# A two-block model on one core: both attentions, the first output product and the state-space outputs in another order

## The reference

```
proj = rms_norm(x) @ w_in;  q, k, v, p = split(proj)            # 8 heads of 128
a = attention(norm(q), norm(k), v, rel_bias)                    # per head
m = mean of p over the last 2, 4, 8, 16 tokens, minus p; @ pool_w; * pool_scale
x = x + concat(a, m) @ w_out                                    # "mix"
x = x + (silu(conv(h @ w_up)[gate]) * conv(h @ w_up)[val]) @ w_down
h = concat(meta, x)                                             # 16 + 256 = 272 tokens
y_a = rmsnorm((ssd forward + ssd backward + D * xs) * silu(z))  # 8 groups of 4 heads
y_b = silu(layernorm(conv31(val * sigmoid(gate)))) * silu(z_b)
h = h + concat(y_a, y_b) @ w_out_2                              # "outa", then "outb"
q, k, v, z = split(rmsnorm(h) @ w_in_o)                         # 32 heads of 64
h = h + (neighbourhood_attention(q, k, v) * silu(z)) @ w_out_o  # "na", then "naout"
out = rmsnorm(h)[meta:]
```

## Time and profile before

| | us |
|---|---|
| three runs, median | 2695.35 |
| the profiled execution, its own time | 2695.7 |
| its span, first to last instruction | 2693.8 |
| PE busy | 2558.0 |
| DVE busy | 1909.6 |
| ACT busy | 1142.4 |
| POOL busy | 408.3 |

### The profile page before, as it was taken

How to read it: one execution, slowest core, us unless ns; L and a number is a source line. 1 busy time by engine, 2 the same in 40 slices (tenths; PEclk the granted TensorE clock), 3 DMA queues, 4 the chain that set the end, 5 groups by cost and what they waited for, 6 DMA issues and landing times.

```text
span 2693.8 us, 57478 instructions
## 1 busy us (share of the span) xinstructions
PE 2558.0 (95%) x19902; PEld 2449.2 (91%) x19902; DVE 1909.6 (71%) x3412; ACT 1142.4 (42%) x1603; POOL 408.3 (15%) x261
## 2 busy tenths in 40 slices
PE   5998999999999999999989899996989999999997
PEld 4997999999999999999977799996989988888887
DVE  5767767777777555588889888888766656666655
ACT  3443344444444444433366533333334433444433
POOL 0000000000000000020057487771000000000100
PEclk7999999999999999999999999997999999999999
DMA  5454455555556566655544355552455544444443
GB/s 209 158 165 138 149 179 187 187 185 185 185 186 198 180 186 182 190 173 164 179 140 143 122 180 172 175 183 95 147 160 158 177 148 136 154 144 150 141 130 131
DMA packets 160394, 441.00 MB, mean 164 GB/s; under 512 B 39248, under 2 KB 56016, under 8 KB 159968
## 3 DMA queue, kind: packets, MB, share of 16 engines
q1 hardware_dynamic: 157760, 431.48, 50.4%
q0 software_dynamic: 2592, 8.98, 1.2%
HBM read 436.67 MB, written 11.08 MB: 166 GB/s over the span
## 4 chain that ended last, share of the span: by engine, by line
PE 78%; DVE 11%; issue 5%; ACT 4%; DVEq 1%; DMA 0%; ACTq 0%; SPq 0%
PE bank L831 24%; PE bank L832 24%; PE bank L833 24%; ACT whi L511 2%; DVE c L1463 2%; PE bank L1083 2%; DVE wlo L1153 2%; PE bank L1068 1%; DVE eb L1536 1%; ACT eb L675 1%; PE bank L1074 1%; DVE pad L1164 0%; DVE c L1461 0%; PE bank L999 0%; ACT sq L520 0%
## 5 line engine op out<-in xcount | busy, mean ns | idle before, releaser
L831 PE MATMUL bank<-xh,whi 128*128 128x256 f32 (+1 forms) x4496 | 1303.7, 290 | 47.4 <-DVE wlo L1153 27.0
L832 PE MATMUL bank<-xl,whi 128*128 128x256 f32 (+1 forms) x4496 | 1286.3, 286 | 0.0
L833 PE MATMUL bank<-xh,wlo 128*128 128x256 f32 (+1 forms) x4496 | 1286.0, 286 | 0.0
L511 ACT CAST whi<-raw 128x1024 fp32r<-128x1024 f32 x785 | 811.4, 1044 | 658.4 <-PE bank L833 628.5
L1153 DVE TENSOR_TENSOR wlo<-raw,whi 128x1024 fp32r<-128x1024 f32 x689 | 843.6, 1234 | 271.2 <-ACT whi L511 256.0
L831 PEld LDWEIGHTS bank<-xh,whi 128*128 128x128 f32 x4496 | 854.9, 190 | 77.9 <-issue 43.8
L833 PEld LDWEIGHTS bank<-xh,wlo 128*128 128x128 f32 x4496 | 855.1, 190 | 0.0
L832 PEld LDWEIGHTS bank<-xl,whi 128*128 128x128 f32 x4496 | 852.7, 190 | 2.2 <-issue 1.9
L831 PE MATMUL bank<-fh,whi 128*128 128x256 f32 x960 | 271.8, 283 | 0.3 <-DVE fl L1338 0.3
L832 PE MATMUL bank<-fl,whi 128*128 128x256 f32 x960 | 271.7, 283 | 0.0
L833 PE MATMUL bank<-fh,wlo 128*128 128x256 f32 x960 | 271.7, 283 | 0.0
(11 more groups left out here) (280 smaller groups left out, 2813.5 us busy)
## 6 DMA issues: line engine op xcount, KB each, us to landing
raw<-w_up SPq DMA_DIRECT2D x176, 512.0 KB, 4.0
raw<-w_na SPq DMA_DIRECT2D x128, 512.0 KB, 3.8
raw<-w_glu SPq DMA_DIRECT2D x96, 512.0 KB, 3.5
raw<-w_down SPq DMA_DIRECT2D x80, 512.0 KB, 4.2
raw<-w_qkvp SPq DMA_DIRECT2D x64, 512.0 KB, 4.1
raw<-w_xbc SPq DMA_DIRECT2D x64, 512.0 KB, 4.1
raw<-w_mix SPq DMA_DIRECT2D x32, 512.0 KB, 3.9
raw<-w_za SPq DMA_DIRECT2D x32, 512.0 KB, 3.8
```

What stands on the lines that cost most here:

```text
L511: A.copy(whi[s][:, :], raw[s][:, :]).then_inc(sem("hi_done"), 1)
L831: T.matmul(out, wh, mh[:, o:o + n], start=start and r == 0, stop=False)
L832: T.matmul(out, wh, ml[:, o:o + n], start=False, stop=False)
L833: ins = T.matmul(out, wl, mh[:, o:o + n], start=False, stop=stop and r == len(kts) - 1)
```

## The change

On PE, the stream of small and large matmuls is rebuilt in both attentions and in `outa`; other engines follow it.

- `p` has a phase of its own ahead (`pin`), and `qkv` now has 6 chunks per head. POOL makes the windowed means during `qkv` and carries the bias rows through memory; their products with `pool_w` stand in the last two heads. The last head's attention stands between the first chunks of `mix`, which begin with the half of the inputs that comes from the means.
- In `mix`, `down` and `naout` the high weights are multiplied with both parts of the activations by one matmul of 512 columns; the two halves of the bank are added by DVE (one more `TENSOR_TENSOR` per output tile).
- `outputs`, `nscores` and `nvalues` alternate between the two heads. All four scores of a pair stand together (after chunk 0), all transposes (after chunk 4) and all values (after chunk 6).
- `outa`: four banks in turn instead of two; POOL splits its weights; DVE's and ACT's share is written out as a list for 16 tiles, with the layernorm's gain and bias taken into ACT's instruction.
- The last pair's attention stands between the first chunks of `naout`.

What the change does to the streams is shown at three places. PE in the loop over pairs of the neighbourhood attention, before: values of the first head, then the transposes of the second (`nps` are probabilities, `nvr` values, `nsc` scores; the square bracket is what an instruction waits for).

The diff, cut to its core:

```diff
@@ on SP and POOL: the bias table and the windowed means
-            sp.wait_ge(sem("brow_ready"), HEADS)
-            sp.dma_start(brows[:, :], btab[:, :]).then_inc(sem("brow_out"), 16)
...
+            pool.wait_ge(sem("brow_ready"), HEADS)
+            G.dma_start(brows[:, :], btab[:, :]).then_inc(sem("brow_out"), 16)
...
+            def window(out, src, lo_, shift, so, ss):
+                gch.link(G.tensor_tensor(p3(out, lo_, 8, META, TOK, so), p3(src, lo_, 8, META, TOK, ss),
+                                         p3(src, lo_, 8, META - shift, TOK - shift, ss), ADD))
...
+            with pool.Fori(0, 4) as i:
+                for j in range(8):
+                    split("outa", i, j)
@@ in product, for mix, down and naout
-                    T.matmul(out, wh, mh[:, o:o + n], start=start and r == 0, stop=False)
-                    T.matmul(out, wh, ml[:, o:o + n], start=False, stop=False)
-                    ins = T.matmul(out, wl, mh[:, o:o + n], start=False,
-                                   stop=stop and r == len(kts) - 1)
+                    if phase in ("mix", "down", "naout"):
+                        both = pb_[:, 0:2 * n].rearrange("p (t n) -> p t n", t=2)
+                        if not last:
+                            T.matmul(both, wh, halves(mh, ml, o, n), start=head, stop=False)
+                        ins = T.matmul(out, wl, mh[:, o:o + n], start=False, stop=False)
+                        if last:
+                            ins = T.matmul(both, wh, halves(mh, ml, o, n), start=False, stop=True)
+                        continue
@@ on PE: qkv, the last head and mix
+                    if jj == 0 and attn:
+                        turn_values(i * 2 + m, i, 3 * m - 1)
+                    if jj == 1 and attn:
+                        scores(i * 2 + m)
...
+            mixing(0, 0, range(8, 16), start=True)
+            turn_values(8, 3, 5)
+            pe.wait_ge(sem("bank_free"), tile("mix", 0, 1) + 1)
+            mixing(1, 0, range(8, 16), start=True)
             scores(8)
+            pe.wait_ge(sem("vq_ready"), 8)
+            mixing(2, 0, range(8, 16), bank[2], start=True)
+            mixing(3, 0, range(8, 16), bank[7], start=True)
             turn_probs(8)
+            pe.wait_ge(sem("y_ready"), 7)
+            mixing(0, 1, range(7), done=False)
             values(8)
@@ on PE: the outputs of the state-space scan
-                for h in range(2):
-                    for n, (t0, o, w_) in enumerate(YSEGS[d]):
+                for n, (t0, o, w_) in enumerate(YSEGS[d]):
+                    for h in range(2):
@@ on PE: outa
-            outa(0)
-            pe.wait_ge(sem("ln_acc"), 2 + 16)
+                    if begin and j == 0:
                         pe.wait_ge(sem("lsum_ready"), 1)
+                        T.matmul(mean, ones[:, :], lsum[:, :], start=True,
                                  stop=True).then_inc(sem("mean_done"), 1)
+            outa(0, True)
+            pe.wait_ge(sem("lacc_ready"), 1)
@@ on DVE: outa
+            for n in range(16):
+                difference(n)
+                if n > 1:
+                    summed(n - 2)
+                if n in (4, 10):
+                    added(n // 6)
...
+            for n, upto in zip(range(2, 16), (0, 1, 3, 5, 6, 8, 9, 11, 12, 13, 14, 15, 16, 16)):
+                while at_ < upto:
+                    branch(at_)
+                    at_ += 1
+                added(n)
@@ on DVE: the residual of mix, down and naout
+                    if phase != "outb":
+                        ch.link(V.tensor_tensor(xt, from_[:, n:2 * n], xt, ADD))
+                    freed(phase, i, k, V.tensor_tensor(xt, from_[:, 0:n], xt, ADD))
@@ on PE: the neighbourhood attention
+            def nscores(i):
+                pe.wait_ge(sem("bank_free"), tile("na", i, 0) + 2)
+                for m in range(4):
+                    b_, h = divmod(m, 2)
+                    o = 64 * h
+                    T.matmul(bank[3 + m][:, 0:TOK], qt[o:o + 64, b_ * P:b_ * P + P], kt_[o:o + 64, :],
+                             start=True, stop=True).then_inc(sem("nscores_done"), 1)
...
+                for n in range(3):
+                    for h in range(2):
+                        ins = T.matmul(bank[7][64 * h:64 * h + 64, 0:SEQ],
+                                       nvr[:, n * P + 64 * h:n * P + 64 * h + 64],
+                                       nps[h][:, n * SEQ:n * SEQ + SEQ], start=n == 0, stop=n == 2)
...
                     if attn and j == 0:
+                        nscores(i)
+                    if attn and j == 4:
+                        nturn(i)
+                    if attn and j == 6:
+                        nvalues(i)
```

More of the change, by code:

```diff
@@ L547, in residual @@
                 else:
-                    with act.Fori(0, 8) as i:
+                    with act.Fori(2 if phase == "mix" else 0, 8) as i:
                         body(i)
@@ L820, in _, with halves, product @@
             pe.sem_inc(sem("chunk_done"), RING)
-            def product(phase, i, j, k, mh, ml, kts, width, off, n, start, stop):
-                if start:
+            def halves(mh, ml, o, n):
+                h, l = mh[:, o:o + n], ml[:, o:o + n]
+                return bass.AP(tensor=h.tensor, offset=h.offset,
+                               ap=[h.ap[0], [l.offset - h.offset, 2], [1, n]])
+            def product(phase, i, j, k, mh, ml, kts, width, off, n, start, stop, to=None, done=True):
+                if start and phase not in ("mix", "outa", "naout"):
@@ L1341, in _ @@
-            dve.wait_ge(sem("bank_free"), tile("pool", 0, 7) + 3)
-            for n in range(8):
-                dve.sem_inc(sem("y_ready"), 1)
+            with dve.Fori(1, 3) as i:
+                ch.begin(i, 14, 1)
+                qkv(i)
+            ch.end(2)
+            qkv(3, pooled=True)
+            ch.end()
+            split("mix", 0, 0)
+            normalized(8)
+            head_out(7)
+            split("mix", 0, 1)
+            values_in(8)
+            softmax_in(8)
+            split("mix", 0, 2)
@@ L1344, in _ @@
+            softmax_out(8)
+            split("mix", 0, 3)
+            split("mix", 1, 0)
+            head_out(8)
+            split("mix", 1, 1)
             ch.end()
```

767 lines of the change are left out of this document (438 added, 329 removed).

## The result

| | before | after |
|---|---|---|
| device time, median of 4 runs | 2695.05 us | 2583.66 us (2581.68 to 2586.24) |
| ratio to before, 95% interval | | 0.9588 (0.9571 to 0.9604) |
| profiled execution, span | 2695.7, 2693.8 us | 2586.24, 2584.4 us |
| predicted | | 2568 (2542 to 2602) |

The account below looks back on a forecast made before the run. PE bounds the kernel, busy 2558.0 of 2693.8 us. Terms -17 - 13.5 - 16 + 1.3 - 1 - 34 - 39 - 8 = -127 from 2695.7 give 2568 us, range 2542 to 2602.

Parts of the forecast that it names:

- Start and first attention to mix: Up to the first sum of squares -17 us (bounds -10, -21); first attention to `mix` -13.5 (bounds -5, -17).
- POOL has made the means during the first heads: First attention to `mix`: the means are off DVE's chain by then; part of the -13.5 us.
- Wide matmul: `mix`, `down`, `naout`: one 512-column matmul for two of 256 gains 13.5 ns a pair, -16 us in all.
- State-space outputs: State-space scan: alternating heads saves perhaps 0.15 us a call over 32 calls; -1 us (bounds 0 and -5).
- what PE saves it then waits: State-space scan: PE waits for DVE, busy 20.63 of 23.40 us a group, so the saving turns into waiting; -1 us.
- outa: First output product: of 46.1 us lost 12 stay, with 7.9 waiting for the sum; -34 us (bounds -20, -38).
- POOL keeps up with a fifth to spare: `outa`: POOL's split takes 2.40 us against 3.02 for a chunk.
- Pairs: Neighbourhood attention: values 1.3, scores 0.9, merging 0.4, so 2.6 us a pair over 15 pairs; -39 (bounds -20, -45).
- Last pair: Last pair's attention between chunks of `naout`, which cover most of the softmax; -8 us (bounds -3 and -9).
- 1.6 stays: Last pair: DVE has some 7.8 us from the first score on, PE has 6.2; 1.6 us of loss remains.
- The shorter heads wait: Rival, first attention: DVE 2 us late in each of 8 heads, 16 us more, 2584; chance 0.12.
- The halves don't overlap: Rival, pairs: only the 0.4 us of a pair is left, 33 us more, 2601; chance 0.08.

Follow-up runs that it names:

- e5: The changed kernel with the windowed means left out, POOL's semaphores kept; single run 2580.51 us.
- e7: The changed kernel with other banks and bank waits in `mix` and `naout`, and the splits of `mix` chunks 9 and 10 moved ahead; 2573.38 us.
- e1: The changed kernel with the state-space outputs run head by head again, not alternating; 2585.09 us.
- e6: The changed kernel with two buffers exchanged in `outa`: the layernorm's running value in PSUM, the gate's output in SBUF; 2582.37 us.
- e11: The changed kernel with all gaining edits together, plus ACT's splits of `outa`'s fourth to sixth chunk ahead of its norm; 2554.08 us.
- e3: The changed kernel with a pair's four score matmuls issued head 0, 0, 1, 1, not alternating; 2586.1 us.
- e8: The changed kernel with the windowed means spread: POOL waits for three more splits of `qkv` before each of twelve portions; 2581.25 us.

## Why the prediction was right, and where it missed

The sum had the sign and the places right, and its parts missed in both directions. The total inside the range owes something to that: the pairs gave 12 us more than forecast, and the first attention, the wide matmul, the scan and the last pair some 29 less. No run takes back the new start, the four banks of `outa` or the place of the last pair alone; their shares are read from the stages before and after.

*Start and first attention to mix, -17 and -13.5.* Short by some 10 us together. The start itself gave 18.5: 73.5 us to the first head's sum of squares, less the 15 chunks of 2.88 us that now stand ahead of it, against 48.8. The stage table's first line has -26.7, and the part of this term that went into `mix` lost 6.5: there the small matmuls (1.3, which the term had counted) and the wait on line 1532 with the clock behind it. The step that failed is "POOL has made the means during the first heads", priced at nothing: I named the work that they hide behind on PE, not what they share with DVE. e5 shows 5.8 us in the first head of after, 3.0 to 5.7 in the other traces. The other step, `mix`'s seam, counted DVE's chain for a head but not the wait for a bank that PE didn't need: 4.4 by e7, with the moved splits in it.

*Wide matmul, -16.* Mechanism right, size off: 7.75 ns a pair and not 13.5, so -9.4. The fixed 13 ns of a matmul were half to be had; 232 ns are 19 above the columns' 213.3, so the surplus of the wide one is larger, if the narrow one beside it kept its own. The forecast's range (0 to 29) held it.

*State-space outputs, -1.* The wrong sign: +4.1 in the scan by e1, 2.8 in the mean over all traces. The step "what PE saves it then waits" was right and stopped one step too early, at the clock behind the longer wait.

*outa, -34.* -34.6, with the 7.8 us for `lsum` as predicted. "POOL keeps up with a fifth to spare" was right for POOL; its splits stayed at 2.4 us. Its price stood on DVE (27.8 us for 16 instructions of 0.44) and cost two waits, 3.0 together. They are put down to POOL, but POOL waited for ACT's copy, which stood behind a gate that waited 4.07 us for DVE, and e6 ended them by freeing DVE. That the total came out at the forecast's -34 is in part luck: e11 shows that another 11 us were to be had.

*Pairs, -39.* -50.9, 3.39 a pair and not 2.6. Values 1.43 (predicted 1.3) and scores 1.10 (0.9): right, taken from the state-space call's row. Under-sized was the merging, 0.4, which measured the rest, 0.86: 0.35 in the transposes (1.58 us a pair before, 1.23 now), 0.14 of idle time that is gone, and the rest at the edges between small matmuls and the stream, of which there are fewer. Right size, wrong reason in part: I put the overlap down to alternation, and e3 shows that for two matmuls a half standing together is enough.

*Last pair, -8.* About -0.4 (-2.4 with `naout`'s wide matmuls, 2.0, in it). The step "1.6 stays" counted DVE's softmax and not the fourth tile's bank: 6.4 us idle and a clock of 0.69 over the 11 us around it, of which e7 gave back 6.0.

*The rivals.* "The shorter heads wait" came true in the first head only, by another mechanism; the next four periods are 19.7 us, and the last two, 24.9, hold the products of the means. "The halves don't overlap" and the slow wide matmul are refuted by the rows above.

*The signs.* Two were worked out wrongly. Line 1031 came first at 92.2 us and not at 48 to 51: I had taken 17 from 67.4 and left out the chunks of `pin` ahead of it. The first wide matmul of `mix` came at 250.9, where my own sum gives 247 and not 240. Two waits of over 1 us stood behind the one for `lsum`, where none should. The pairs (27.98 us), the six value matmuls (1.45), the one long wait for `lsum` and the groups of the scan (23.2 us apart, with longer waits for `eb`) came as said or better.

## What to carry to other kernels

When an output tile is given a bank, write down which tile PE will wait for when that bank comes round: the end of `naout` lost 6 us to a wait for a neighbour's bank, and `mix` part of its 4, with nothing wrong in the amount of work. Work moved to POOL is not free because POOL is idle: look for DVE instructions that read only SBUF beside it, and cut the work in pieces or put one input into PSUM. And make no engine faster that then only waits: when the wait grows, the clock behind it can cost more than was saved. And before a gain of a few microseconds is read from one pair of traces, look at the same stage in every trace that left it alone.

## What the hardware showed that was not expected

- Two halves of the array overlap without alternation, two matmuls deep: 1.45 us alternating, 1.93 head by head, 2 x 1.44 apart (values); 1.12, 1.12 and 2 x 1.11 (scores). The depth is read from one order of three matmuls a half and fits the one of two; longer rows of matmuls weren't tried.
- A POOL instruction of 2.4 or 3.6 us holds up a DVE instruction until it ends, if all that this one reads lies in SBUF; one PSUM input frees it (1739 ns against 441 in the mean of 16). A PSUM output doesn't (1230). POOL waits for DVE in the same way (3.61 against 2.75 us).
- The same wait in the scan was followed by a granted clock of 0.69 over 10.4 us in after (2.37 us of idle time) and of 1.00 in e8 (2.38 us).
- The surplus of an fp32r matmul over its columns: 13 ns at 256 and 272 columns, 19 at 512 (worked out from the 352.1 ns of a wide and a narrow one together).
